# One weight stream for attention and project, delta scalars in project, bias rows in prepare

## The reference, cut to what matters

```
h   = layer_norm(x);  ada = silu(c) @ w_ada + b_ada     # 6 rows of 1024: shift, scale, gate (twice)
u   = h * (1 + sc1) + sh1
proj = u @ w_in        # qkv_a (3072), z, b_a (8), a_a (8), q_b (1024), k_b, v_b (128 each), two gates
qkv_a = silu(causal_depthwise_conv(qkv_a, conv_w));  q_a, k_a = l2_normalize(...)
beta = sigmoid(b_a);  g = -exp(a_log) * softplus(a_a + dt_bias)
gc   = cumsum of g inside chunks of 64 tokens;  decay = exp(gc_i - gc_j)
o_a  = gated_delta_rule(q_a, k_a, v_a, g, beta)          # 8 heads, 16 chunks in sequence
y_b  = window_attention(q_b, k_b, v_b, sinks, rel_bias)  # 16 heads; logits + bias by distance
mix  = (sigmoid(gate_a) * y_a + sigmoid(gate_b) * y_b) @ w_out
h    = layer_norm(alpha * h + gt1 * mix);  then routed experts, and a last layer_norm
```

## Time and profile before

| | |
|---|---|
| median of 3 runs | 2120.18 us (2119.71 to 2122.32) |
| the profiled execution | 2119.42 us, its span 2117.6 us |
| PE busy | 1843.7 us (87%) in 14118 matmuls |
| DVE busy | 1438.9 us (68%) |
| ACT busy | 1048.1 us (49%) |
| mean granted clock | 0.937 |

### The profile page before, as it was taken

The page is one execution under the profiler, slowest core; times in us unless marked ns, Lnnn a source line. Parts: engine busy times, 40 slices in busy tenths (PEclk is TensorE's granted clock), DMA queues, the critical chain, the costliest instruction groups (busy, mean ns, idle before and its releaser), DMA issues. The chain is left out here.

```text
span 2117.6 us, 35235 instructions
## 1 busy us (share of the span) xinstructions
PE 1843.7 (87%) x14118; PEld 1041.4 (49%) x14118; DVE 1438.9 (68%) x1829; ACT 1048.1 (49%) x1266; POOL 370.9 (18%) x251
## 2 busy tenths in 40 slices
PE   4668987999973999986999999649999999999955
PEld 0345653434433999984444445424544445444422
DVE  3425564765654666652675668769999998888927
ACT  0425563344422324233333331119888888888934
POOL 0000000011101122120000000013444444444400
PEclk9789998999985999998999999759999999999987
DMA  8430007454434413103232312239999999999925
GB/s 340 82 99 1 1 1 257 149 180 176 153 120 127 107 47 92 48 2 121 72 100 84 116 40 87 110 140 394 392 405 417 411 401 401 391 390 394 357 106 204
DMA packets 167441, 397.82 MB, mean 188 GB/s; under 512 B 25289, under 2 KB 104450, under 8 KB 139530
## 3 DMA queue, kind: packets, MB, share of 16 engines
q1 hardware_dynamic: 149386, 353.90, 46.3%
q0 software_dynamic: 17920, 42.02, 5.1%
HBM read 361.68 MB, written 55.16 MB: 197 GB/s over the span
## 5 line engine op out<-in xcount | busy, mean ns | idle before, releaser
L2094 PE MATMUL ps<-w_gate_up_split,gathered_t 128*128 128x512 f16 x1728 | 387.0, 381 | 5.2 <-ACT gathered_t L2158 4.4
L2227 DVE SCALAR_TENSOR_TENSOR w_gate_up_split<-w_staged,w_gate_up_split 128x2048 f16<-128x2048 f32 x144 | 327.9, 2289 | 53.4 <-ACT w_gate_up_split L2149 52.1
L2149 ACT ACTIVATE w_gate_up_split<-w_staged 128x2048 f16<-128x2048 f32 x144 | 274.3, 1908 | 66.6 <-PEq L144 30.5
L2094 PEld LDWEIGHTS ps<-w_gate_up_split,gathered_t 128*128 128x128 f16 x1728 | 167.5, 98 | 204.3 <-ACT gathered_t L2158 6.7
L751 PE MATMUL ps<-u_transposed,w_qkv_split 128*128 128x512 f16 x1152 | 254.2, 383 | 13.9 <-DVE w_qkv_split L844 13.9
L187 PE MATMUL ps<-u_transposed,w_gates_split 128*128 128x512 f16 x1152 | 250.6, 379 | 0.0
L2121 PE MATMUL ps<-w_down_split,hidden_t 128*128 128x512 f16 x864 | 195.7, 384 | 7.3 <-ACT hidden_t L2195 4.1
L751 PEld LDWEIGHTS ps<-u_transposed,w_qkv_split 128*128 128x128 f16 x1152 | 112.7, 99 | 159.0 <-DVE w_qkv_split L844 15.1
L187 PEld LDWEIGHTS ps<-u_transposed,w_gates_split 128*128 128x128 f16 x1152 | 112.6, 98 | 138.4 <-issue 3.8
L2227 DVE SCALAR_TENSOR_TENSOR w_down_split<-w_staged,w_down_split 128x2048 f16<-128x2048 f32 x72 | 164.2, 2287 | 19.7 <-ACT w_down_split L2149 19.2
L2149 ACT ACTIVATE w_down_split<-w_staged 128x2048 f16<-128x2048 f32 x72 | 137.2, 1908 | 46.0 <-DMA w_staged<-in_w_down 22.5
(11 more groups left out here) (356 smaller groups left out, 2888.5 us busy)
## 6 DMA issues: line engine op xcount, KB each, us to landing
w_staged<-in_w_gate SPq DMA_DIRECT2D x72, 1024.0 KB, 11.4
w_staged<-in_w_up SPq DMA_DIRECT2D x72, 1024.0 KB, 10.7
w_staged<-in_w_down SPq DMA_DIRECT2D x72, 1024.0 KB, 10.3
w_ada_ring<-in_w_ada SPq DMA_DIRECT2D x8, 2048.0 KB
w_qkv_ring<-in_w_in SPq DMA_DIRECT2D x12, 1024.0 KB, 6.7
qkv_scratch<-qkv_silu POOLq DMA_DIRECT2D x24, 512.0 KB, 3.0
qkv_tile<-qkv_scratch SPq DMA_DIRECT2D x8, 1536.0 KB, 8.4
w_gates_ring<-in_w_in SPq DMA_DIRECT2D x24, 512.0 KB, 6.4
```

Of the source, the lines that this page charges most:

```text
L2094: last = pe.matmul(ps[:, GU[s] + j, :], xt[:, s, xp, k, :], w16[:, j, wp, k, :], start=(k == 0 and t == 0), stop=(k == KC - 1 and t == 2))
L2149: nc.scalar.activation(split(kind, 0, int(q)), staged(m, kind, int(q)), ACT.Identity, scale=W_SCALE).then_inc(hi_ok[kind + q], 1)
L2227: nc.vector.scalar_tensor_tensor(split(kind, 1, int(q)), staged(m, kind, int(q)), W_SCALE, split(kind, 0, int(q)), ALU.mult, ALU.subtract) ...
```

## The change

1. `prepare` loads `rel_bias` and the first two weight pieces of attention, right behind `w_ada`; PE sums the bias rows between `columns(0)` and `ada(2)`, DVE copies them ahead of `part`, SP stores them, and `small_rows` comes after that store.
2. Attention and project share one ring of two slots (`w_ring`, `w16`), one stream of 17 pieces: 0 to 4 are attention's, 5 to 16 project's. Pieces 5 and 6 are split in attention's loop at steps 16 and 24.
3. `project` starts with pieces 5 and 6 split. It computes the token scalars: beta and exp(a_log) behind pair 5, the softplus behind pair 7, the sums of decays between pairs 9 and 10, the decay rows behind pair 10; POOL stores them at pair 11. The pieces of late `ada` are loaded and summed in another order: 4 and 5 are loaded at pairs 6 and 7, and piece 7 is summed at pair 10, in a bank and a row buffer of its own. The squares of the keys use the space of `m.yb`, after its store.
4. `delta_rule` has no head left: SP loads the decays of pair 0 first, then q, k and v in two DMAs.

```diff
+def load_dense(m, a, sp, i):
+    ...
+        at = QB0 + (i - 1) * 2 * P if i < 5 else (i - 5) * 2 * P
+        sp.dma_start(m.w_ring[:, i % 2, :, 0:2 * P], w[:, :, at:at + 2 * P]).then_inc(m.w_in[i % 2], 16)
+def split_dense_high(nc, m, act, i):
+    n = WIDE if i == 0 else 2 * P
+    act.wait_ge(m.w_in[i % 2], (i // 2 + 1) * 16 + (16 if i % 2 == 0 else 0))
+    nc.scalar.activation(m.w16[:, i % 2, 0, :, 0:n], m.w_ring[:, i % 2, :, 0:n], ACT.Identity, scale=W_SCALE).then_inc(m.w_hi, 1)
+def split_dense_low(nc, m, dve, i):
+    n = WIDE if i == 0 else 2 * P
+    dve.wait_ge(m.w_hi, i + 1)
+    nc.vector.scalar_tensor_tensor(...).then_inc(m.w_lo, 1)
 # prepare, SP
                 sp.dma_start(wada[:, n], ...)
+            sp.dma_start(rel[:], a["rel_bias"]).then_inc(rel_in, 16)
+            load_dense(m, a, sp, 0)
+            load_dense(m, a, sp, 1)
+            sp.wait_ge(bias_rows, 1)
+            sp.dma_start(m.bias_dram..., rel_rows...to_broadcast([QH, P, 320])).then_inc(m.bias_out, 16)
             sp.dma_start(m.small[:], a["small"].to_broadcast([P, 72])).then_inc(small_in, 16)
             sp.wait_ge(small_in, 16)
 # prepare, PE
             columns(0)
+            pe.wait_ge(rel_in, 16)
+            pe.matmul(ps[0:QH, 5, 0:320], rel[:], m.const("one_hot", BUCKETS), start=True, stop=True).then_inc(bias_mm, 1)
             ada(2)
 # prepare, DVE
+            dve.wait_ge(bias_mm, 1)
+            nc.vector.tensor_copy(rel_rows[:], ps[0:QH, 5, 0:320]).then_inc(bias_rows, 1)
             dve.wait_ge(wada_in[EARLY - 1], 16)
 # attention, SP
+            sp.wait_ge(m.bias_out, 16)
+            sp.dma_start(bias[:], ...).then_inc(bias_in, 16)
+            for i in range(2, 7):
+                sp.wait_ge(m.w_lo, i - 1)
+                load_dense(m, a, sp, i)
 # attention, ACT (and DVE alike with split_dense_low)
-                if t == TC:
-                    split_high(4)
+                if t in (TC, 2 * TC, 3 * TC):
+                    split_high(3 + t // TC)
 # project
-    ADA_AT = {p: n for n, p in enumerate((0, 1, 2, 3, 8, 9, 10, 11))}
+    ADA_AT = {0: (0,), 1: (1,), 2: (2,), 3: (3,), 8: (4,), 9: (5,), 10: (6, 7)}
+        sq = m.yb[:, 0:2, :]
 # project, SP
-            load(0)
-            load(1)
             load_ada(0)
-                n = {4: 2, 5: 3, 6: None, 9: 4, 10: 5, 11: 6}.get(p)
+                n = {4: 2, 5: 3, 6: 4, 7: 5, 11: 6}.get(p)
 # project, PE, extras(p)
+                if p == 8:
+                    pe.wait_ge(g_ok, 1)
+                    ... (four matmuls of 64 columns).then_inc(sums_mm, 1)
+                if p == 9:
+                    pe.wait_ge(tab_ok, 1)
+                    pe.transpose(ps[0:TC * H, 5, 0:P], sc[:, 3]..., m.const("ident")).then_inc(gc_t, 1)
+                    pe.wait_ge(ssq_in, 16)
+                    pe.transpose(ps[:, 6, 0:TC * H], ssq_rows[:], ...).then_inc(ssq_t, 1)
 # project, ACT, behind silus(p)
+                if p == 5:
+                    (Sigmoid to BETA, Exp of a_log)
+                if p == 6:
+                    act.wait_ge(xa, 2)
+                    (Exp)
+                if p == 10:
+                    act.wait_ge(gc_t, 1)
+                    (Exp, Identity, Exp, Exp, Exp).then_inc(exp_ok, 1)
+                    act.wait_ge(ssq_t, 1)
+                    (Sqrt).then_inc(root_ok, 1)
 # project, DVE
+                if p == 11:
+                    key_scalars()
                 convolve(p)
+                if p == 10:
+                    partial(LATE - 1)
+                for n in ADA_AT.get(p - 1, ()):
+                    row(n)
+                if p == 5: softplus_arguments()
+                if p == 7: log_decays()
+                if p == 9: decay_sums()
 # delta_rule, SP
-            sp.dma_start(ssq[:], ...)
-            load_qkv(0)
-            load_qkv(1)
-            sp.wait_ge(S("gc_row_ok"), 2)
-            sp.dma_start(m.gc_dram, gc_rows).then_inc(S("gc_out"), 16)
-            sp.wait_ge(S("gc_out"), 16)
             load_decays(0)
+            load_qkv(0)
             load_decays(1)
+            load_qkv(1)
```

338 lines of the change are left out of this document (163 added, 175 removed).

## The result

The changed kernel takes 2103.1 us (median of 4 runs, 2098.2 to 2107.6) beside 2121.1 for the kernel before on the same chip: a ratio of 0.9915, 95% interval 0.9898 to 0.9932. It is 18 us faster; 29.3 were forecast, and 2103 lies outside the range of 2081 to 2101. Repeated later it gave 2103.1 again (5 runs, 2099.0 to 2105.0).

A forecast was written before the change was run, and what follows sets the result against it. TensorE works 87% of the span, but four waits up to 675 us were what the change could shorten. Terms 6.4 + 0 - 6.3 - 7.8 + 9.7 - 10.1 + 1.0 - 11.4 - 10.8 = -29.3 gave 2091 us, range 2081 to 2101.

The forecast's parts named there:

- The split at step 24: Attention's loop: ACT's copy, then its high and low halves, delay the mask of step 25; +5.2 us.
- What bounds the kernel: Up to 675 us: four gaps stand, two of PE's 8.26 and 10.42 us; in project itself PE is the bound.
- prepare: Block prepare: PE waits for `rel_bias` ahead of `ada(2)`, +6.4 us; the store ahead of `small_rows` 0, up to +5.
- the opening: Attention's opening: weights are already there, so ACT splits at 77.3 instead of 83.6 of the old clock; -6.3 us.
- the bias load: Attention: bias loaded at the opening, so DVE's 7.81 us idle goes whole; -7.8 us.
- Two splits in the loop: Attention's loop: +4.5 us for step 16 and +5.2 for step 24, together +9.7, bounds 8 to 12.5.
- Project opens with two pairs split: Project's first half: the 10.42 us wait shrinks to about 1.0 and PE stays off the low clock; -10.1 us stays.
- Scalars in project: Project: small PE matmuls and transposes cost +1.0 us; DVE and ACT work fits their idle time.
- Project's tail: End of project: the last `ada` piece needs no stored row, the last convolution is 10.2 us earlier; -11.4 us.
- delta_rule without a head: delta_rule's start: `lower` 11.8 us behind the opening, before 22.65; -10.8 us, what follows moves as a block.
- given back in project: Rival: project's DVE and SP chain yields only 5 of 10.1 us, an ACT group holds one pair by 3; 2099, chance 0.12.
- The clock rival: Rival: the granted clock in experts falls, at 0.92 costing 39 us, 2130; chance 0.04, shared with an unseen stall.

The follow-up runs named there:

- e1: The changed kernel with the sixth dense piece split as project opens, not at step 24 of attention's loop: 2093.5 us, ratio 0.9867.

## Why the prediction was wrong

The time came out 11.3 us above the forecast. Two steps of the prediction failed most. The split at step 24 was priced at 5.2 us, ACT's and DVE's work, without the clock; it costs 7.7 to 9.6. And q and k were to land 9 to 10 us behind delta_rule's opening, with all that follows moving as a block; they landed at 11.2, and the solver behind them took longer. With two smaller ones the misses are 2.5 to 4.4 (step 24), 2.3 (project's first half), 2.0 to 2.3 (second half and tail) and 3.7 to 4.1 (delta_rule): 10.5 to 13.1 together.

- **What bounds the kernel, prepare, the opening, the bias load:** right, -6.1 and -8.4 in the two profiles for -7.7. `rel_bias` landed at 50.4 (forecast 50.0), the opening at 85.0 (83.6), the bias addition without a wait. The store was hidden by a hair as said: `small_rows`, behind it, landed at 81.9, and with `ada(2)` not late it became the bound (81.0).
- **Two splits in the loop:** step 16 was right (4.5 forecast; 24.28 for four steps, once 19.8), since the row it was read from holds the same gap and the same low clock. Step 24 is the first step that failed. I priced it as ACT's and DVE's 4.2 us plus a little, since "nothing of q is left for PE to do beside it", and did not ask what the gap does to the clock. Taking the split away gives 9.6 us, adding it to the kernel before costs 7.7. Some 2.5 to 4.4 us of the miss.
- **Project opens with two pairs split:** the 10.42 us wait went, as forecast, but 7.7 of the 10.1 stayed. The gain of a first pair on the high clock was right: up to the first sum of late `ada` the products took 41.5 us and not 43.7, 2.2 for the 2.1 forecast (the working as written, 41.85 less 39, gives 2.9). I named the right wait (457.6) and the wrong pace: the third pair's weights, which the two experiments with them show to be worth 0 to 3.5. The pace is the circle of rows. From the opening, the sixth pair moved by 8.7 us, and its products began on the low clock. 2.3 us.
- **Scalars in project:** beside the products 1.0 was forecast and 1.4 measured. At the tail the key scalars had 1.5 in the tail's sum, and taking all scalars away shortens it by 1.8. So this part was sized nearly right; 0.4 us. No drain showed behind the table loads: they take 1.28 us and the next operation follows, which the Trainium skill, ScalarE: Activation LUTs, "What ACT_TABLE_LOAD costs", would have made 2.66.
- **Project's tail:** right in mechanism. The step "that piece needs no stored row" is worth 10.6 us in time and 11.8 in the trace. The 9.8 and 9.5 of the profiles are 1.6 to 1.9 less than forecast: in the first profile the last convolutions start 9.4 us earlier against PE's last product, and not 10.2, and from POOL's last issue to the opening it takes 7.7 us, where I had left the 6.9 as it was. The order of the pieces, which I had not separated, is worth nothing that shows.
- **delta_rule without a head:** forecast 10.8, measured 9.4 at `lower` and 7.1 at the first state product. q and k were issued 2.8 us behind the opening and landed 11.2 behind it, not at 9 to 10, and the solver behind `lower` then lost 1 to 3 us, in the two profiles of this kernel most of it the stop without a releaser. My sentence that "what follows" is "a chain fed by its own stages and moves as a block" failed here. 3.7 to 4.1 us.
- **The rivals:** "given back in project" is the nearest (it gave 2.3 of its 5 us, and no pair ended late for an ACT group), but the largest loss was not on the list. The clock rival looked for the grant in experts, where it did not fall (0.98 before, 0.99 in both profiles after); it fell in attention.

## What to carry to other kernels

Before putting 4 us of other engines' work into a loop that PE shares with them, look at whether PE has products beside it: where it has none, price the gap and also one to four steps on the low clock behind it (a row from a place where PE has products, as step 8, doesn't tell that price), or move the work to a place where PE runs alone, as beside project's first pair. A ring with one place too few hides well: the wait for a stored row did not look like a pace in the rows on which I built, and cost project 10.6 us at its end and, at the other rows, 8.8 more. Sum what a part gives and costs before it is made: the scalars, some 8 us of forecast in three places, were worth 3.0 in time and 5.0 in the trace.

## What the runs showed of the hardware that I had not expected

- One gap of 4.14 us on PE, with PE some 60% busy ahead of it, brought the granted clock to its low level each time, in all six profiles with this split; on the low level the same stretch of work lasted from one to four steps. The gaps of 4.09 us did the same, at step 8 in all 18 profiles and at step 16 in the 15 with a split there; with products of q behind them one step was slow (7.08 us for 5.44 at step 16) and the next was not. With PE filled behind the gap at step 24 it lasted one step (one profile). The 1.76 us for which PE is held at the first step of a set brought it down at times: at step 24 never, at step 16 in the kernel before (the scores at 249.67 take 1.65 us) and in its copy with the split, at step 8 in three profiles.
- In the solver of delta_rule's first pair PE stopped for 0.4 to 3.4 us inside a group of matmuls, with nothing it waited for, in 13 of the 15 profiles without the scalars at the head and in none of the 3 with them. In the profile after, the DMA share ahead of it was 1.05 to 1.19, but in e1, which had no stop, it was 1.12 too. The trace has one thing more: a packet of 16 KB on the queue that it calls "instruction" starts 20 to 25 us behind the opening in all 15, and in the 13 within 2.5 us of the stop's beginning; in the 3 with a head it starts 30 us behind the opening, when the tiles have landed and the DMA share is 0.02. That PE stopped for instructions which came late is the nearest reading. It isn't shown: two kernels have the packet and no stop, and no experiment was made on it.
- A stage moved in which no instruction was changed: from merge's opening to the end the changed kernel took 2.5 us more in one profile and 0.1 us more in the other than the kernel before. In the 18 profiles this part lasts 1128.8 to 1134.7 us, and the kernel before with the split at step 24 takes as long there as the longest of the changed one (1134.7), so the 2.5 us are drift of the executions and not shown to be the change's.
